# A dense expert layer: scores made inside the query projection, heads ranked one by one, 64 more tokens' gates by indirect transfers

## The reference, cut to what matters

```python
def peer_ffn(h, w_q, sub_keys, u_tab, v_tab):
    q = (h @ w_q).reshape(B, L, PEER_HEADS, 2, PEER_HALF)
    s = jnp.einsum('blhpd,pnd->blhpn', q, sub_keys)
    top_s, top_i = lax.top_k(s, PEER_TOPK)                 # 16 of 128, twice
    cand_s = top_s[..., 0, :, None] + top_s[..., 1, None, :]
    cand_i = top_i[..., 0, :, None] * PEER_NKEYS + top_i[..., 1, None, :]
    best_s, best_pos = lax.top_k(cand_s.reshape(B, L, PEER_HEADS, PEER_TOPK * PEER_TOPK), PEER_TOPK)
    idx = jnp.take_along_axis(cand_i.reshape(...), best_pos, axis=-1)
    gate = jax.nn.softmax(best_s, axis=-1)
    ...
        act = gelu(einsum('bpd,bphkd->bphk', h, u_tab[idx]))
        coef = act * gate
        out = einsum('bphk,bphkd->bpd', coef, v_tab[idx])
```

## Time and profile before

| | |
|---|---|
| time, median of 3 runs | 2508.28 us (2502.68 to 2514.2) |
| profiled execution, its own time | 2508.97 us |
| its span | 2507.2 us |
| PE busy | 2356.0 us (94%) |
| DVE busy | 1620.3 us (65%) |
| ACT busy | 1220.1 us (49%) |
| POOL busy | 426.1 us (17%) |
| DMA | 422.64 MB, mean 169 GB/s |

### The profile page before, as it was taken

One profiled execution on the slowest core, in us unless ns is written; L12 is line 12 of the kernel. 1 busy time (PEld: TensorE's weight loads), 2 busy tenths in 40 slices (PEclk: granted clock), 3 DMA queues, 4 the chain that ended last, 5 costly groups with the idle time before them and its releaser, 6 DMA issues.

```text
span 2507.2 us, 47024 instructions
## 1 busy us (share of the span) xinstructions
PE 2356.0 (94%) x14990; PEld 2095.7 (84%) x14990; DVE 1620.3 (65%) x3530; ACT 1220.1 (49%) x2592; POOL 426.1 (17%) x262
## 2 busy tenths in 40 slices
PE   7989999999997899999899999999999996999998
PEld 2767789999997788888668777789999996888887
DVE  2465346887877777777215674346887868777776
ACT  1355235555557555555123522045555557555554
POOL 0000000267673000000000000000376771000000
PEclk9998999999999999999999899999999999999999
DMA  6476454677772466666243322454677771566664
GB/s 236 154 232 210 159 167 160 180 181 185 184 178 63 151 213 211 215 210 211 93 144 123 103 85 93 143 176 160 183 181 182 185 183 23 189 207 208 209 210 162
DMA packets 190941, 422.64 MB, mean 169 GB/s; under 512 B 54256, under 2 KB 89328, under 8 KB 190208
## 3 DMA queue, kind: packets, MB, share of 16 engines
q1 hardware_dynamic: 149824, 413.73, 50.3%
q0 software_dynamic: 36864, 0.15, 4.6%
q10 hardware_dynamic: 4160, 7.64, 0.9%
HBM read 403.48 MB, written 17.96 MB: 168 GB/s over the span
## 4 chain that ended last, share of the span: by engine, by line
PE 88%; DVE 7%; issue 2%; ACT 2%; DMA 0%; ACTq 0%; DVEq 0%; PEld 0%; PEldq 0%
PE ps L716 20%; PE ps L1376 19%; PE ps L1370 11%; PE ps L1371 11%; PE ps L1372 11%; PE ps L1377 10%; PE ps L801 2%; DVE arena L1655 1%; DVE gbuf L1621 1%; PE ps L1062 1%; PE ps L1040 1%; PE ps L1646 1%; PE ps L1408 1%; DVE gbuf L813 0%; DMA ring<-stream 0%
## 5 line engine op out<-in xcount | busy, mean ns | idle before, releaser
L1376 PE MATMUL ps<-csplit,hl 128*128 128x512 f32 x2048 | 719.9, 396 | 7.0 <-DVE hl L1695 7.0
L1589 POOL DMA_INDIRECT gates<-gbuf,picks_at x256 | 425.2, 1661 | 1658.9 <-DVEq L1558 1485.6
L1370 PE MATMUL ps<-hsplit,hl 128*128 128x256 f32 x2304 | 655.7, 285 | 9.6 <-DVE hsplit L910 4.6
L1371 PE MATMUL ps<-hsplit,hl 128*128 128x256 f32 x2304 | 653.7, 284 | 0.0
L1372 PE MATMUL ps<-hsplit,hl 128*128 128x256 f32 x2304 | 653.7, 284 | 0.0
L1377 PE MATMUL ps<-csplit,hl 128*128 128x256 f32 x2048 | 575.6, 281 | 0.0
L1447 ACT CAST hl<-ring 128x512 fp32r<-128x512 f32 x562 | 347.8, 621 | 356.7 <-PE ps L1372 315.6
L1450 DVE TENSOR_TENSOR hl<-ring,hl 128x512 fp32r<-128x512 f32 x562 | 389.5, 693 | 199.8 <-ACT hl L1447 158.5
L1376 PEld LDWEIGHTS ps<-csplit,hl 128*128 128x128 f32 x2048 | 385.4, 188 | 97.9 <-issue 7.3
L716 PE MATMUL ps<-arena,ring 128*128 128x256 f32 (+2 forms) x1896 | 446.3, 395 | 15.6 <-issue 8.8
L1370 PEld LDWEIGHTS ps<-hsplit,hl 128*128 128x128 f32 x2304 | 443.9, 193 | 11.2 <-issue 10.7
(11 more groups left out here) (199 smaller groups left out, 1802.6 us busy)
## 6 DMA issues: line engine op xcount, KB each, us to landing
ring<-stream SPq DMA_DIRECT2D x723, 512.0 KB
gates<-zeros SPq DMA_DIRECT2D x32, 512.0 KB, 5.0
gring<-gates SPq DMA_DIRECT2D x256, 64.0 KB, 2.9
gates<-gbuf,picks_at POOLq DMA_INDIRECT x256
arena<-keys ACTq DMA_DIRECT2D x2, 1024.0 KB, 4.9
gbuf<-consts ACTq DMA_DIRECT2D x1, 1120.0 KB, 5.0
arena<-xT ACTq DMA_DIRECT2D x1, 1024.0 KB, 11.7
arena<-ctxT ACTq DMA_DIRECT2D x1, 1024.0 KB, 13.8
```

The lines of the kernel that those rows point to most:

```text
L1370: pe.matmul(out_ap, w[0], m[0], start=start, stop=False)
L1371: pe.matmul(out_ap, w[1], m[0], start=False, stop=False)
L1376: pe.matmul(ps[:, bank, :], w_hi, m_both, start=start, stop=False)
L1589: pool.indirect_dma_start(out=cells, out_offset=bass.IndirectOffsetOnAxis(ap=picks_at[:, i, c:c + 1], axis=0), in_=gates[:, i, c:c + 1], i ...
```

## The change

- **Scores** are made head by head inside the `wq` units (`pe_scores`, `act_scores`): four matmuls a head behind every second unit.
- **Ranking** begins in `wq` unit 7, and goes head by head, both token halves of a head together: 2 x 10 slots of `topk_part` and 10 of `lookup_part`, 30 slots a head, 240 in all.
- **Transfers.** Tokens 128 to 191 go to the DRAM table too. Their 64 values of an even head and 64 of an odd head are paired into one transfer of 128; the odd head's are moved to partitions 64 to 127 by two small transfers that ACT issues (`act_pair`). A block has 128 + 64 = 192 indirect transfers where it had 128. A head's 16 wait only for the heads before it, a pair's 16 only for the pairs before it.
- **The one-hot stage** makes the last 64 tokens: 8 groups.
- **The table** is 256 wide: tokens 0 to 191, then the odd heads' 64. Zeroing takes 32 pieces a block, one after every second unit, and the second block's begin earlier. A slice is 128 KB, and DVE adds its last 64 columns to the 64 before them (`add_pair`, for unit n+3) before `multiply`, now 192 wide.

```diff
-    def peer_pe_scores(pe, b):
-        pe.wait_ge(S("u_bank_free"), banks_freed(b, "u") + 4)
-        pe.wait_ge(S(f"keys_loaded{b}"), 16)
+    def pe_scores(pe, b, h):
+        pe.wait_ge(S("u_bank_free"), banks_freed(b, "wq") + 4 + 2 * h + 2)
+        wait(pe, "peer_s_copied", HEADS * (b - 1) + h - 3)
...
+        def send_head(h):
+            pool.wait_ge(S("picks_ready"), HEADS * (b - 1) + h + 1)
+            wait(pool, "head_sent", 16 * TOPK * ((b - 1) * HEADS + h))
+            for k in range(TOPK):
+                send(picks_at[:, h, k:k + 1], gates[:, 0, h * TOPK + k:h * TOPK + k + 1], "head_sent")
+        def send_pair(j, half):
+            if half == 0:
+                pool.wait_ge(S(f"paired{j}"), 32 * b)
+                wait(pool, "pair_sent", 16 * TOPK * ((b - 1) * HEADS // 2 + j))
+            for k in range(half * TOPK // 2, (half + 1) * TOPK // 2):
+                send(pair_at[:, j, k:k + 1], pair_g[:, j, k:k + 1], "pair_sent")
...
-    ZERO_PARTS = 16
-    ZERO_EVERY = 3
+    ZERO_PARTS = 32
+    ZERO_EVERY = 2
...
-    NG = P // 8
+    NG = STAGED // 8
...
+    def add_pair(dve, b, i, s):
         at = s % GATE_RING
         dve.wait_ge(S(f"gates_in{at}"), i * 16 + 16 * ((b - 1) * N_IT + s // GATE_RING + 1))
-        c = ds(i * (UB * T) + s * T, P)
-        dve.tensor_tensor(acts[:, c], acts[:, c], gring[:, at, :], ALU.mult).then_inc(S("gate_applied"), 1)
+        dve.tensor_tensor(gring[:, at, P:SENT], gring[:, at, P:SENT], gring[:, at, SENT:T], ALU.add)\
+           .then_inc(S("pair_added"), 1)
+    def multiply(dve, b, i, s):
+        dve.wait_ge(S("pair_added"), i * UB + ((b - 1) * P + s + 1))
+        c = ds(i * (UB * T) + s * T, SENT)
...
+                if kind == "dve" and not (last and s >= UB - 3):
+                    add_pair(eng, b, i, s + 3)
                 if kind == "dve" and not (last and s >= UB - 2):
                     multiply(eng, b, i, s + 2)
...
-                sp.wait_ge(S("scattered"), 16 * b * HEADS * TOPK)
+                sp.wait_ge(S("head_sent"), 16 * b * HEADS * TOPK)
+                sp.wait_ge(S("pair_sent"), 16 * b * HEADS // 2 * TOPK)
...
-            for b, key in ((1, "fill1"), (2, "gv")):
+            for b, key in ((1, "fill1"), (2, "cq")):
```

More of the change, by code:

```diff
@@ L57 @@
 ZEROS = 512
+EXTRA = 64
+SENT = P + EXTRA
 NPROJ = 3
@@ L1514, in lookup_part @@
     def lookup_part(eng, b, i, n):
-        best = picks_best[:, i, :].rearrange("p (m k) -> p m k", k=TOPK)
-        g4 = gates[:, i, :].rearrange("p (m k) -> p m k", k=TOPK)
-        row = slice(i % 2 * 64, i % 2 * 64 + 64)
+        row = slice(i * TOPK, (i + 1) * TOPK)
+        g2, cell = gates[:, :, row], cell_f[:, :, :]
+        ranks = (rank1, rank2)
         if n == 0:
@@ L1553, in lookup_part @@
[L1553 to L1560, removed]
-        eng.drain()
+                eng.tensor_reduce(chosen[:, x, :, row], hit.rearrange("p (t k) a -> p t k a", t=NT), AX_X, ALU.add)
@@ L1574, in pe_turn @@
-        for c, rows in enumerate((chosen[:, 0, :], chosen[:, 1, :], late)):
+        pe.wait_ge(S("picks_ready"), HEADS * b)
+        for c, rows in enumerate((chosen[:, 0, 1, :], chosen[:, 1, 1, :], gates[:, 1, :])):
             mm = pe.transpose(ps[:, 4, c * P:(c + 1) * P], rows, ident)
@@ L1581, in pool_scatter, with send @@
         pool.wait_ge(S(f"zeroed{b}"), 16 * ZERO_PARTS)
[L1582 to L1593, removed]
-    ZERO_PARTS = 16
-    ZERO_EVERY = 3
-    PER_ZERO = P * P // ZEROS // ZERO_PARTS
+        def send(where, what, done):
+            pool.indirect_dma_start(out=cells, out_offset=bass.IndirectOffsetOnAxis(ap=where, axis=0), in_=what,
+                                    in_offset=None, compute_op=ALU.add, bounds_check=P * P * T - 1,
+                                    oob_is_err=True).then_inc(S(done), 16)
+        def send_head(h):
[9 more added lines that the diff above has]
+                send(pair_at[:, j, k:k + 1], pair_g[:, j, k:k + 1], "pair_sent")
+        send_head(0)
+        for j in range(HEADS // 2):
+            send_head(2 * j + 1)
+            send_pair(j, 0)
+            if j + 1 < HEADS // 2:
+                send_head(2 * j + 2)
+            send_pair(j, 1)
+    ZERO_PARTS = 32
+    ZERO_EVERY = 2
+    PER_ZERO = P * T // ZEROS // ZERO_PARTS
     def zero_part(eng, b, n):
@@ L1710, in v_loop @@
         if kind == "dve":
+            for s in range(3):
+                add_pair(eng, b, 0, s)
             for s in range(2):
@@ L1722, in peer_pe @@
         pe.drain().then_inc(S("split_used"), HLRING - EARLY)
-        for s in range(1, UB):
[L1724 to L1728, removed]
+        for s in range(1, NQ):
+            u_unit("pe", pe, b, 0, s, table="wq")
+            if s == 3:
+                pe.wait_ge(S(f"keys_loaded{b}"), 16)
+            if s >= 3 and s % 2 == 1:
+                pe_scores(pe, b, (s - 3) // 2)
+        u_unit("pe", pe, b, 0, 0)
+        pe_scores(pe, b, HEADS - 1)
+        for s in range(1, UB):
             u_unit("pe", pe, b, 0, s)
@@ L1749, in peer_act @@
         enter_act(act, b)
-        for s in range(UB):
+        for s in range(NQ):
             u_unit("act", act, b, 0, s, first=True, table="wq", ready=EARLY)
-        u_loop("act", act, b, 1, NQ // UB, table="wq")
+            if s >= 5 and s % 2 == 1:
+                act_scores(act, b, (s - 5) // 2)
         early_hi(act, b, 0, "u")
```

178 lines of the change are left out of this document (101 added, 77 removed).

## The result

The changed kernel takes **2570.22 us** in the median (2568.22 to 2572.24, 4 runs) against 2505.48 before: ratio 1.0256, 95% interval 1.0234 to 1.0277. It is slower, as forecast and inside the range, but by 65 us and not by 117. The profiled execution has a span of 2566.4 us against 2507.2, 59.2 longer.

A forecast was written before the change was run, and what follows sets the result against it. PE, holding 88% of the span, was taken as the bound, with POOL bounding the v loops' start after the change. 2509 + 22 + 19 + 41 + 30 + 5 = 2626 us; the 8-in-10 range was 2540 to 2670.

The forecast's parts named there:

- circle over two units: V loop: split, issue, landing, addition, multiply and splits of unit n+2 take 6.2 us per two units, 3.10 a unit.
- the rival with the table in time: Transfers at 1.96 us each let PE start the v loops 20 us earlier, but the loops are slowed; 2545 us, chance 0.10.
- the forecast's own case: POOL's transfers delay the v loops' start and the slices' wait slows the loops; 2575 to 2690 us, chance 0.70.
- v loops: +41 and +30 forecast: V loops of blocks 1 and 2 slow to 3.10 and 3.05 us a unit, against 2.77 and 2.81, over 124 units.
- The start: +22 and +19 forecast: V loops begin at 854 and 2155 instead of 832 and 2136, because POOL's 176 transfers from the second head on end late.
- they come regularly, at every 15th and every 28th transfer by count, so I keep them: POOL's 11 long gaps without a releaser in the trace stay, giving 2.20 us a transfer in block 1, 2.18 in block 2.
- The head waits: POOL's seven waits for a head's landing, 21.6 us in block 1, go; worth 0.15 us a transfer.
- Zeroing: +5 forecast: 16 more pieces of 512 KB a block cost 5 us in block 1 (0 to 15) and 0 in block 2.
- Scores at nothing: Score matmuls moved into the projection, with ACT's copies and DVE's ranking beside PE, cost 0; bounds 0 to 8 us.
- landings are quick: Rival: landings of 2.5 us or less keep PE's 2.77 a unit and the table in time; 2474 us, chance 0.10.
- The port pair: GpSimd cannot write descriptors while DVE holds the shared ports; one-hot overlap costs some 5 us, idle time returns 3, taken to cancel.
- the 1.84 from start to start with DVE idle: By the port rule alone, POOL's last 20 transfers run at 1.84 us and the v loop starts 7 us earlier a block.

The follow-up runs named there:

- late-addition version: Changed kernel with the addition of a slice's last 64 columns moved from three units ahead to two, directly before the multiply; 2504.61 us, ratio to before 0.9979.

## Why the prediction was right, and where its sizes were off

**The direction and both mechanisms held; one size did not.** The wait moved one unit forward closes a circle over two units, and POOL became the bound of the v loop's start. But it became the bound at the old start, not 20 us after it, and all that made the kernel slower lies in the v loops. The time is inside the range for 8 in 10, which reached down to the rival with the table in time, and below the 2575 at which the forecast's own case began. The order of one passage of the circle can be read in the changed kernel's chain, from one issue to the next but one:

```profile
1002.18 0.33 SPq L1927
...
1002.77 2.90 DMA gring<-gates
...
1006.18 0.42 DVE csplit L1730
1006.60 1.22 DVE hl L1733 x2
...
1007.97 0.33 SPq L1927
```

5.79 us for two units, with PE's matmuls nowhere in it.

**v loops: +41 and +30 forecast, +31 and +30 measured.** The circle averaged 3.02 and 3.08 us a unit where I had 3.10 and 3.05. In the passage shown the landing took 2.90 to 3.0 (the median is 3.1; I took 3.2). And not every slice closes the circle fully. In block 2 the agreement of +30 is partly luck: the loop of before took 363 us there, at the slower pace, and 357 in other executions.

**The start: +22 and +19 forecast, -3.5 and -3.6 measured**, counted from each block's own projection (832.0 - 345.5 and 2136.4 - 1650.3 before, 830.9 - 347.9 and 2165.2 - 1682.7 after). This is the term that was mis-sized. The step that failed is "they come regularly, at every 15th and every 28th transfer by count, so I keep them". I read a period off one program and took it for a property of the transfers. It depends on the space for descriptors (25, 11 and 2 gaps with 2048, 4096 and 6144 bytes) and on the order of the transfers (20 gaps with pairs last). In the changed kernel there were 9 after the second head's first, not 15. They were shorter too, 2.3 us on average where the eleven of before were 2.9. So a transfer took 2.06 us, not 2.20, over 175 transfers 24 us. The lower end of my own range, 2.07, was close to the true value. The head waits did go, as forecast.

**Zeroing: +5 forecast; +6 (2 to 10) alone.** In the changed kernel the projection began 2.4 us later, 347.9 for 345.5, in this one execution. In the others with the larger table it began at 345.7 to 354.4, in those with the smaller one and half the zeroing at 341.1 to 345.5.

**Scores at nothing: right.** Their matmuls stand inside the units, PE is busy for all of the u loop, and from the projection's first matmul to the u loop's last it takes 1 us less than before. **The rival "landings are quick" failed** on the row it was held against: no landing between 900 and 1200 us was shorter than 2.8 us. **The rival "the table is in time"** was right in its half, that the start would not be late against before, but wrong in its price: at 2.06 us a transfer there is no gain either.

The sum by measured terms: 2.4 for the first projection, -3.5 and -3.6 for the starts, 30.7 and 30.5 for the v loops, and 2.8 for the stretch from block 1's last v matmul to block 2's projection (461.8 before, 464.6 after), for which I had no term. That is 59.3, the difference of the two spans.

The port pair, which the prediction weighed by the Trainium skill (page "SBUF — State Buffer", section "SBUF: two separate sides"), was not needed for the long gaps. In the late-addition version all but one of ten vanished with 6144 bytes, while DVE's ranking stayed as it was. In the changed kernel 16 transfers took 1.68 us on average beside the one-hot stage, and the last ten, with DVE idle, 1.55. That is 2 us for the stage where I had 5; the 1.84 from start to start with DVE idle came as estimated, at 1.85.

## What to carry to other kernels

When a wait is moved earlier, write down the circle it closes: what it waits for, what set that off, and how many iterations lie between. One line moved by one iteration, with no work or byte added, cost 14 and 13 us in the two loops.

An engine that is hidden has an unmeasured price. POOL ran 300 us unseen; put on the path, its gaps decided when the v loop began, and 2048 more bytes a partition for its descriptors took 26 us off the late-addition version.

Before a period seen in a trace is carried over to other code, ask what resource makes it, and change that resource once.

## What the runs showed that was not expected

- The space for the descriptors of indirect transfers sets POOL's pace: with 128 values a transfer, 25 gaps among 192 transfers with 2048 bytes, 11 with 4096, 2 with 6144, one of each being the wait for the second head and the others 1.8 to 4.2 us long. Leaving out the waits for a head or a ranking, block 1's first long gap stands at the 8th, 16th and 23rd transfer, and in the kernel before, with 4096 and 6144 bytes, at the 16th and 23rd too. From that I estimate some 256 bytes a transfer. From the second head on a transfer took 2.25, 2.06 and 1.97 us. The last transfer of block 1 started at 859.0, 827.0 and 807.6. That the gaps are waits for landed transfers to free room fits this, but no row names what POOL waits for, and the eight gaps that stayed in the kernel before with 6144 bytes are not explained by it.
- A v loop in which PE waits for nothing has two paces at a granted clock of 0.99 to 1.00. A unit takes 2.77 or 2.83 us, steadily through the loop but for its first units, and a loop about 357 or 363. The matmul of 512 columns takes 391 or 398 ns in the median. The kernel before had the first in block 1 and the second in block 2, with more zeroing it was the other way round, and with 6144 bytes both were quick. No row shows what sets the pace, and a difference of 6 or 7 us between two single profiles may be no more than this.
- A slice of 64 KB landed 2.9 to 3.0 us after issue behind 512 KB of weights, one of 128 KB 3.1, and one of 128 KB issued ahead of the weights again 3.1 in the median, from 1.9 to 4.3.
- An indirect transfer with 128 values costs POOL 1.55 us in the median and a gap of 0.30 at the least; the mean was 1.66 beside the ranking.
